# The first half of both input projections by seven half-size products per pair of chunks, and scores on 64 rows

## The reference

```
h = rms_norm(x) * gain * (1 + sc1) + sh1
z = h @ w_in          # columns: q 512 | k 512 | v 512 | pool input u 512 | gates 2048
q, k = rms_norm per 64-wide map (4 heads x 2 maps)
s = q k^T / 8 + relative bias, softmax per map; a = p0 - lam * p1; o = a v
y_pool = trailing-window means of u, minus u, times w_pool
x = x + gt1 * ((g0 * (o @ w_b1) + g1 * (y_pool @ w_b2)) @ w_out)
x = x + gt2 * ffn(h2)   # layer 0: dense SwiGLU; layer 1: 2 of 8 experts
```

## Time and profile before

| | |
|---|---|
| times of three runs | 1604.09, 1604.80, 1605.57 us (median 1604.8) |
| span of the profiled execution | 1600.4 us; no time outside the span is recorded for it |
| median of the runs minus the span | 4.4 us |
| PE busy | 1562.8 us, 98% of the span |
| DVE busy | 553.8 us, 35% |
| chain that ended last | PE 85%, DMA 11%, DVE 3% |
| HBM | 517.47 MB read, 333 GB/s over the span |

### The profile page before, as it was taken

How to read it: one execution, slowest core, us unless ns; L and a number is a source line. 1 busy time by engine, 2 the same in 40 slices (tenths; PEclk the granted TensorE clock), 3 DMA queues, 4 the chain that set the end, 5 groups by cost and what they waited for, 6 DMA issues and landing times.

```text
span 1600.4 us, 37215 instructions
## 1 busy us (share of the span) xinstructions
PE 1562.8 (98%) x16734; PEld 1007.7 (63%) x16734; DVE 553.8 (35%) x1210; ACT 179.5 (11%) x478; POOL 69.5 (4%) x118
## 2 busy tenths in 40 slices
PE   7999999999999999999999999999999999999997
PEld 3778898999997888944444444444554555555544
DVE  4468378666555784751101100110111011101133
ACT  2102303111112032131000000000000000000000
POOL 1110500000000110010000000000000000000010
PEclk9999999999999999999999999999999999999999
DMA  9999869666359746569999999999999999999995
GB/s 362 364 386 344 296 230 320 230 225 216 127 178 319 234 156 193 166 224 405 418 418 405 418 418 403 418 417 405 418 404 418 417 398 415 408 405 417 408 386 191
DMA packets 174340, 535.30 MB, mean 334 GB/s; under 512 B 12535, under 2 KB 101413, under 8 KB 161378
## 3 DMA queue, kind: packets, MB, share of 16 engines
q1 hardware_dynamic: 158706, 497.20, 81.1%
q0 software_dynamic: 8768, 28.96, 5.2%
q10 hardware_dynamic: 6704, 6.72, 1.3%
HBM read 517.47 MB, written 15.82 MB: 333 GB/s over the span
## 4 chain that ended last, share of the span: by engine, by line
PE 85%; DMA 11%; DVE 3%; issue 1%; ACT 1%; SPq 0%; DVEq 0%
PE bank L1877 31%; PE bank L1898 15%; PE bank L1191 14%; PE bank L1552 14%; DMA ring<-in_w_exp_up 8%; PE bank L1462 2%; PE bank L1732 2%; PE bank L1223 1%; DMA ring<-in_w_in 1%; DVE inv L2511 1%; PE bank L1719 1%; PE bank L1567 1%; DMA ring<-in_w_ada 1%; PE bank L1645 0%; DMA area<-in_w_exp_down 0%
## 5 line engine op out<-in xcount | busy, mean ns | idle before, releaser
L1877 PE MATMUL bank<-ring,xT 128*32 128x448 f32 x3072 | 301.2, 539 | 6.4 <-DMA ring<-in_w_exp_up 6.4
L1877 PE MATMUL bank<-ring,area 128*32 128x448 f32 x3072 | 300.8, 539 | 1.5 <-DMA ring<-in_w_exp_up 1.4
L575 DVE TENSOR_TENSOR area<-bank,area 128x448 f32<-128x448 f32 x48 | 46.0, 958 | 575.0 <-ACT area L1149 575.0
L1552 PE MATMUL bank<-hT,ring 128*128 128x264 f32 x1024 | 239.4, 389 | 4.0 <-ACT hT L892 3.7
L1898 PE MATMUL bank<-area 128*32 128x256 f32 x3840 | 225.6, 379 | 1.3 <-DMA area<-in_w_exp_down 1.3
L1552 PEld LDWEIGHTS bank<-hT,ring 128*128 128x128 f32 x1024 | 193.3, 191 | 38.9 <-issue 6.9
L1877 PEld LDWEIGHTS bank<-ring,xT 128*32 128x32 f32 x3072 | 109.8, 110 | 166.0 <-issue 157.7
L1877 PEld LDWEIGHTS bank<-ring,area 128*32 128x32 f32 x3072 | 109.5, 110 | 161.7 <-issue 154.6
L1898 PEld LDWEIGHTS bank<-area 128*32 128x32 f32 x3840 | 138.1, 110 | 99.6 <-issue 41.6
L1149 ACT ACTIVATE area<-bank 128x448 f32<-128x448 f32 x48 | 26.1, 544 | 778.8 <-PE bank L1877 778.8
L1898 PE MATMUL bank<-ring,area 128*32 128x256 f32 x1536 | 89.2, 379 | 0.6 <-DVE area L583 0.6
(11 more groups left out here) (367 smaller groups left out, 1273.0 us busy)
## 6 DMA issues: line engine op xcount, KB each, us to landing
ring<-in_w_exp_gate SPq DMA_DIRECT2D x128, 896.0 KB, 17.3
ring<-in_w_exp_up SPq DMA_DIRECT2D x128, 896.0 KB, 19.2
area<-in_w_exp_down SPq DMA_DIRECT2D x64, 1024.0 KB, 18.6
ring<-in_w_ada SPq DMA_DIRECT2D x96, 512.0 KB, 9.0
ring<-in_w_in SPq DMA_DIRECT2D x32, 1024.0 KB, 13.2
ring<-in_w_exp_down SPq DMA_DIRECT2D x32, 1024.0 KB, 19.6
area<-in_w_exp_down SPq DMA_DIRECT2D x32, 512.0 KB, 19.5
ring<-in_w_ff_gate SPq DMA_DIRECT2D x11, 1024.0 KB, 6.2
```

What stands on the lines that cost most here:

```text
L575: dve.tensor_tensor(F["act_tok"][:, t, :].rearrange("p (i n) -> p n i", i=BODY), bank[3 + t][:, 0:SLICE].rearrange("p (n i) -> p n i", i=B ...
L1552: mm = pe.matmul(bank[b][:, 0:T], w[:, c, :], hT[:, c, :], start=(c == 0), stop=(c == DC - 1))
L1877: mm = pe.matmul(bank[t + 3 * half][32 * g:32 * g + 32, 0:SLICE], tokens[:, t, 32 * r:32 * r + 32], w[half][:, SLICE * g:SLICE * (g + 1)], ...
```

## The change

The first half of the projection, chunks 0 to 15, is computed in eight units of two chunks, `Z_UNITS = 8`, in both layers. The gate chunks 16 to 31 stay as they are.

- **PE:** per unit seven products of four 128x128x132 matmuls, in the order 1, 2, (4 of the unit before), 6, 5, 7, 3. The layer-0 `modulation` calls stand behind product 4.
- **DVE:** per unit four weight sums `sum_z`, three adds out of PSUM (`z11`, `z12`, `z22`) and one copy (`z21`), in place of two copies of whole chunks (three operations per chunk for the pool input); and once per layer four sums of halves of `hT` (`sum_h_z`). All eight `past_scores` calls now stand behind the last unit.
- **ACT:** per unit three copies out of PSUM (`z_one`, `z_two_five`). It takes over from DVE the five copies of bias rows in layer 0 and the copies of the attention output (`read_o`).
- **Queries:** stored once in `q_n`, with one multiply per chunk. The zero fills of `qz` go away. A score is two matmuls on 64 rows each, one per map, into two banks (4 and 5, or 6 and 7).
- **Banks:** attention turns and outputs all use bank 0; sample scores, key turns and the `comb_m` products use bank 1; the new pool rows use bank 6, so `score(1)` waits for `read_new`. The key turns move from chunks 24 and 26 to 20 and 22.
- **POOL:** its early input loads wait for the first pages to be freed, which is now at product 4 of unit 0. Its wait for the bias rows is one count higher.
- The counts of semaphores of later stages shift by the eight units.

```diff
+Z_UNITS = 8
...
-        STATE_AT = (5, 7)
+        STATE_AT = (2, 3)
...
-            pool.wait_ge(s.bias_out, H)
+            pool.wait_ge(s.bias_out, H + 1)
...
+                for u in range(Z_UNITS):
+                    z_one(u)
+                    if 2 <= u < 6:
+                        root_qk(2 * u - 4)
+                        root_qk(2 * u - 3)
+                    if 1 <= u < 5:
+                        square_qk(2 * u - 2)
+                    z_two_five(u)
+                    if 1 <= u < 5:
+                        square_qk(2 * u - 1)
...
+                    if n == 1:
+                        pe.wait_ge(s.vs_out, 2 * l + 2)
                     if n >= 2:
                         pe.wait_ge(s.score_out, 8 * l + n - 1)
                     for m in range(2):
-                        mm = pe.matmul(bank[4 + n % 2][:, m * S:m * S + w], ATT["qz"][:, m, h, i * P:(i + 1) * P],
-                                       ATT["kT"][:, h, 0:w], start=True, stop=True)
+                        r = slice(m * HD, (m + 1) * HD)
+                        mm = pe.matmul(bank[4 + 2 * (n % 2) + m][:, 0:w], ATT["q_n"][r, h, i * P:(i + 1) * P], ATT["kT"][r, h, 0:w],
+                                       start=True, stop=True)
...
+                def z_six_five(u):
+
+                    done = z_units_of[l]
+                    pe.wait_ge(s.w_summed, z_summed(l, u, 1))
+                    pe.wait_ge(s.one_kept, done + u + 1)
+                    if u == 0:
+                        pe.wait_ge(s.h_summed, 12 * l + 2)
+                    product(z_left(u), z_w(u, 1), z_h(1), False).then_inc(s.product_mm, 1)
+                    pe.wait_ge(s.c11_read, done + u + 1)
+                    product(z_right(u), z_w(u, 0), z_h(0), True).then_inc(s.product_mm, 1)
...
+                for u in range(Z_UNITS):
+                    z_first(u)
+                    z_second(u)
+                    if u:
+                        z_fourth(u - 1)
+                    z_six_five(u)
+                    z_seven_three(u)
+                    if l == 0 and u in STATE_AT:
+                        turn_state(STATE_AT.index(u))
+                    if 1 <= u < 5:
+                        sum_qk(2 * u - 2)
+                        sum_qk(2 * u - 1)
+                    if u == 5:
+                        turn_sample_queries()
+                    if u == 6:
+                        turn_sample_keys()
+                z_fourth(Z_UNITS - 1)
...
-                    step(dve.memset(ATT["qz"][HD:P, 0, :, :], 0.0))
-                    step(dve.memset(ATT["qz"][0:HD, 1, :, :], 0.0))
...
+                sum_h_z(0)
+                sum_h_z(1)
+                for u in range(Z_UNITS):
+                    if u:
+                        z12(u - 1)
+                    if l == 0 or u == 0:
+                        sum_z(u, 0)
+                        sum_z(u, 1)
+                    z11(u)
+                    if u:
+                        z21(u - 1)
+                    sum_z(u, 2)
+                    sum_z(u, 3)
+                    if u == 0:
+                        sum_h_z(2)
+                        sum_h_z(3)
+                    if 2 <= u < 6:
+                        norm_qk(2 * u - 4)
+                    if u == 6:
+                        read_sample_queries()
+                    if u == 7:
+                        read_sample_keys()
+                    z22(u)
+                    if l and u < Z_UNITS - 1:
+                        sum_z(u + 1, 0)
+                        sum_z(u + 1, 1)
+                    if 2 <= u < 6:
+                        norm_qk(2 * u - 3)
...
+                    if u == 5:
+                        early_mod()
+                    if u == 6:
+                        last_inputs()
+                z12(Z_UNITS - 1)
+                z21(Z_UNITS - 1)
+                past_scores(0)
+                past_scores(1)
```

More of the change, by code:

```diff
@@ L941, in read_a, with read_o @@
                         act.wait_ge(s.av_mm, 4 * l + h - 1)
[L942 removed]
+                    act.copy(ATT["aT"][:, h % 2, :], bank[0][:, 0:384]).then_inc(s.aT_out, 1)
+                def read_o(h):
+                    act.wait_ge(s.av_mm, 4 * l + h + 1)
+                    act.copy(oT[:, h, 0:S], bank[0][:, 0:S]).then_inc(s.o_out, 1)
                 def read_pool(g):
@@ L967, in _ @@
                         read_pool(g - 13)
+                read_o(3)
                 read_pool(3)
@@ new lines, in z_first @@
+                def z_first(u):
+                    w, arrived, count = z_page(l, u)
+                    unit[u] = w
+                    pe.wait_ge(arrived, count)
+                    if u >= 2:
+                        pe.wait_ge(s.z_out, ZC * l + 2 * (u - 2) + 2)
+                    if l == 0 and u == 1:
+                        pe.wait_ge(s.bias_out, 2)
+                    for c in range(4):
+                        if u == 0:
+                            pe.wait_ge(s.h_ready, 2 * DC * l + c + 1)
+                        mm = pe.matmul(z_left(u), w[:, c, 0:P], hT[:, c, 0:HALF], start=(c == 0), stop=(c == 3), skip_group_check=True)
+                    mm.then_inc(s.product_mm, 1)
@@ new lines, in z_second, with z_w, z_h @@
+                def z_second(u):
+                    if u == 0:
+                        pe.wait_ge(s.h_ready, 2 * DC * l + DC)
+                    product(z_right(u), [unit[u][:, 4 + c, 0:P] for c in range(4)], [hT[:, 4 + c, 0:HALF] for c in range(4)],
+                            True).then_inc(s.product_mm, 1)
+                def z_w(u, k):
+                    return [zw_sum[:, u % 2, k, c, :] for c in range(4)]
+                def z_h(k):
+                    return [zh_sum[:, k, c, :] for c in range(4)]
@@ new lines, in z_seven_three @@
+                def z_seven_three(u):
+                    done = z_units_of[l]
+                    pe.wait_ge(s.w_summed, z_summed(l, u, 3))
+                    pe.wait_ge(s.two_kept, done + u + 1)
+                    if u == 0:
+                        pe.wait_ge(s.h_summed, 12 * l + 3)
+                    product(z_left(u), [unit[u][:, c, P:2 * P] for c in range(4)], z_h(2), False).then_inc(s.product_mm, 1)
+                    pe.wait_ge(s.five_kept, done + u + 1)
+                    product(z_right(u), z_w(u, 2), [hT[:, 4 + c, HALF:T] for c in range(4)], False).then_inc(s.product_mm, 1)
@@ new lines, in sum_qk, with turn_sample_queries @@
+                def sum_qk(j):
+                    if l == 0 and j == 0:
+                        pe.wait_ge(s.bias_out, H + 1)
+                    pe.wait_ge(s.qk_square, 8 * l + j + 1)
+                    if j >= 2:
+                        pe.wait_ge(s.qk_root, 8 * l + j - 1)
+                    pe.matmul(bank[6 + j % 2][:, 0:T], halves, sq[:, j, :], start=True, stop=True).then_inc(s.qk_sum_mm, 1)
+                def turn_sample_queries():
+                    pe.wait_ge(s.qk_ready, 8 * l + QC)
+                    pe.wait_ge(s.qk_root, 8 * l + 7)
+                    for h in range(H):
+                        t = pe.transpose(bank[6][0:NS, h * P:(h + 1) * P], ATT["q_n"][:, h, S:T], ident)
+                    t.then_inc(s.qs_mm, 1)
```

398 lines of the change are left out of this document (212 added, 186 removed).

## The result

The changed kernel takes 1614.2 us (median of 4 runs, 1613.3 to 1615.9) beside 1605.2 us for the kernel before on the same chip. The ratio is 1.0055 with a 95% interval of 1.0042 to 1.0067, so 9 us are lost. The prediction was 1607.5 us with a range of 1600.5 to 1612.5: the sign was the forecast's, the size was not, and the time lies outside the range.

What follows compares the result with a forecast made beforehand. In the projection's first half PE bounds layer 1 and DMA layer 0; with the change DVE's chain holds PE up. Layer 0's -0.3 and layer 1's +3.0 give +2.7 on 1604.8: 1607.5 us, range 1600.5 to 1612.5.

Steps and rivals of the forecast that it cites:

- The walk: Layer 1's projection, PE, DVE and ACT lists stepped against each other: 8.5 us of PE waits for 6.6 us saved.
- DVE's unit at 7.8 us: Layer 1, units 2 to 5: DVE needs 7.8 us a unit against PE's 7.2, longer by 0.6.
- The announced idle PE: Layer 1: PE waits for DVE, 1.7 us over units 3 to 5, 2.0 in unit 6, 0.8 in unit 7.
- the 62 to 65 announced: Sign in layer 1: chunk 16 starts 62 to 65 us after product 1.
- the forecast 97.3 to 98.3: Layer 0, unit 6: DVE's copy of the sample queries starts at 97.3 to 98.3 us, before it was 92.90.
- PE's clock halves in layer 1's head (0.10): Rival, chance 0.10: one stretch at half clock in layer 1's head costs at most 1.7 us, total 1609.2.
- The scores were taken at 0.43 us: Both layers: a wide score takes 0.43 instead of 0.86 us; only the last one's 0.43 per layer comes through.
- Chunk 16's page would land at about 113: Layer 0: chunk 16's page lands at about 113 us, some 1.7 earlier, since query broadcasts come later.
- PE idle before the `comb_m` products: Sign in layer 1: PE waits before the `comb_m` products until 597.2, released by DVE, 3.3 us late.
- PE keeps the pace: Rival, chance 0.14: DVE needs under 7.2 us a unit, 7 to 9 us are saved, total about 1597.
- The broadcasts come later still: Rival, chance 0.15: query broadcasts take 11 instead of 8 us, each layer loses 2.5 to 3 more, about 1613.
- Nothing moves: Rival, chance 0.06: the same DVE chain levels both layers, earlier cache loads give back 3 us, total 1604.8.

Runs made afterwards that it cites:

- fill_head: Changed kernel plus eleven matmuls per layer, results unread, filling PE's idle time in unit 0; ratio 1.0049 to the kernel before.
- u_layer1: Changed kernel with products in layer 1 alone and plain chunks back in layer 0; ratio 1.0049 to the kernel before.
- score_128: Changed kernel with each half of a score contracting over all 128 rows instead of 64; ratio 1.0067 to the kernel before.
- u_layer0: Changed kernel with products in layer 0 alone and plain chunks back in layer 1; ratio 1.0014 to the kernel before.
- new_early: Changed kernel with `read_new` placed before `past_scores(6)` in DVE's list instead of behind it; ratio 1.0051 to the kernel before.
- two_fill: Changed kernel with unit 1's products 1 and 2 before unit 0's product 6 in layer 1, idle matmuls in both heads; ratio 1.0030 to the kernel before.
- recip_fill: fill_head with the reciprocal of every query and key norm over 32 of 264 columns, both layers; ratio 1.0014 to the kernel before.
- short_sums: Changed kernel with layer 1's third and fourth weight sum per unit over 16 of 128 columns; ratio 1.0050 to the kernel before.
- q_early: Changed kernel with layer 1's sample queries turned in unit 4 and copied in unit 5, one unit earlier; ratio 1.0067 to the kernel before.

## Why the prediction failed

**The mechanism** was the right one. Products add more to DVE than they take from PE, the cached-key products move from three microseconds before chunk 16 to behind it, and the layers are levelled at the `comb_m` products. The walk put the first product 6 at 490.05, which is 492.52 with the later start, measured 492.64; DVE's unit at 7.8 us, measured 7.82. The announced idle PE was there in units 3 to 5 (0.23 us each), 6 (1.30 us, released by DVE's L2462) and 7 (0.53). Chunk 16 came 65.0 us after product 1, at the far end of the 62 to 65 announced, and 63.9 in fill_head, where 63.5 was forecast. That the query copy of layer 0 came at 98.28, inside the forecast 97.3 to 98.3, is luck: the forecast had no slower clock in it, and in fill_head the copy came at 96.31. Taken as a whole, the profiled execution of fill_head is the kernel that I had forecast, one whose clock does not fall in layer 1: layer 0 +0.8 and layer 1 +3.8 us, against -0.3 and +3.0. Its median is still 7.9 us above the kernel before, so the agreement holds for its fastest execution.

**The step that failed** is the granted clock, "PE's clock halves in layer 1's head (0.10)". I had costed the new head's idle time as waits alone, in both layers. The clock fell in both: 6.8 us longer in layer 0 and 6.8 us in layer 1, and filling the heads brought back 1.7 and 1.75 us in the profiled execution. That the forecast's price of a dip (1.7) agrees with this is luck: it was half of 3.4 us, all of it on products, and the dip was 6.8 us long, part of it on waits. Too small was the chance, and wrong were the assumptions that there would be one dip, in one layer, of one size; even that rival's 1609.2 lies 5 us under the result. With 10.2 us in the head and 3.4 more behind `score(1)`, as u_layer1 and score_128 show, layer 1 loses 8.8 to 9.3 and not 5.5 us. I had also held layer 0's head to be covered by its pages. It is not, since the slow head delays the queries' copy by 2.0 us (98.28 against 96.31 in fill_head), and the copy sets the broadcasts.

Of the 6.3 us between the forecast's +2.7 and the 9.0, these 3.4 are the largest part; 1.9 are the smaller terms below, by fill_head's layers, and 1.0 lies behind both layers. This split is the profiled executions'. By the medians fill_head gives back 1.0 us, and how much of the 6.3 the clock makes in a typical execution is open.

**Smaller terms.** The scores were taken at 0.43 us; they cost 0.63 and 0.20 behind, so the 0.43 us that I counted for each layer behind the `comb_m` products did not come. This makes up about half of the 1.9. The broadcast in layer 0 took 9.3 us and not 8.4, and waits for cached keys were 2.9 us there and 2.45 in layer 1, where they had been 1.6 and 1.8; the first cached-key product of layer 0 came at 113.69 and not 112.2. "Chunk 16's page would land at about 113" was wrong for this execution: PE started it at 115.33, released by its page, where it was 114.93. In u_layer0 and score_128, with the same code in layer 0, it started at 113.5 and 113.7 without a wait for its page, and the branch hardly moved (194.40 and 195.03). And of the 4.4 us between the span and the median of the kernel before, which the sum carries over, only about 1.7 are the time outside the span; the rest is that one fast execution.

**The wait at score(1)** was said to be levelled later, and new_early shows it. But I had listed as a sign "PE idle before the `comb_m` products", and it is absent in the changed kernel: the earlier wait had already used it up. It also had a price that I did not see, since a dip followed it in u_layer1, score_128, two_fill and recip_fill (waits of 2.0 to 2.3 us), though none followed the wait of 2.0 us in short_sums. In layer 0 the waits at `score(1)` were 1.8 to 2.5 us in four kernels (changed, u_layer0, score_128, q_early), and only the 2.1 us of q_early were followed by one.

**The rivals.** "PE keeps the pace" is refuted twice over: DVE's 7.8 us held, and recip_fill, which gives it the DVE that it asked for, still does not reach the time of before. "The broadcasts come later still" holds for layer 0 only, by 0.9 us. In layer 1 the first landed at 550.2, before DVE wanted it at 552.5. "Nothing moves" is out.

## What to carry to other kernels

When PE is relieved by giving another engine work, look for the first operation of that engine that is in line behind the new work, and measure from there to the point where both meet: here keys + 78.5 us gave layer 1's time of seven kernels within 0.6 us, and chunk 16's earlier start in recip_fill did not help. A new wait at the head of a stage costs more than its length where it lets PE's clock fall: 1.75 us more in layer 1's head. Here it was filled with the next unit's products or with idle matmuls at no cost that could be seen. Moving one 0.2 us copy to an idle engine, one call forward in a list and two products forward, with a filled head, took back about 8 of 9 us. And one profiled execution does not price a dip: the five of fill_head have spans from 1604.7 to 1609.4 us.

## What was not expected of the hardware

- The same instructions in layer 1's head ran at 1.2 GHz for 6.8 us (changed, new_early, q_early), for 10.2 us (u_layer1, score_128) or not at all (short_sums, whose wait before product 6 was the longest, 1.7 us). The executions of the kernels with products in layer 1 scatter over 1.7 to 8.5 us, with a filled head (3.6 to 6.4) as with an unfilled one, and those without over 1.9 to 4.1. That the clock is the reason is not shown.
- A matmul pair on 64 rows each in two banks takes 0.63 us in place of 0.86 for 256 columns, 0.42 in place of 0.44 for 128, and the matmuls on 128 rows behind it start or end 0.1 to 0.2 us later.
- The first reload of a cached key in layer 1, 256 KB, took 2.9 to 3.1 us in the kernels with plain chunks there, where a page of 1 MB was issued 1.9 us behind it, and 5.7 to 7.0 us in those with products, where the page was issued 0.7 to 1.6 us before it. Later reloads took 2.9 to 7.2 us in either.
